# Two attentions as one pipeline, its first round inside a convolution unit, with shared norm splits: one Trainium2 core

## The reference

```python
m  = silu(c) @ w_mod + b_mod            # six modulation vectors; the same for c_ctx
h  = rms_norm(x,  norm1_g) * (1 + sc1) + sh1
hc = rms_norm(ctx, norm1_g) * (1 + csc1) + csh1      # 256 context tokens
# w_in gives, of h: gqa q, k, v; neighbourhood q, k, v; fourier; conv (a, b); 4 gates of 1024
y_gqa = gqa_latent(q, k, v, kc, vc)                  # 8 heads, 768 keys, softmax
y_na  = neighbourhood_latent(nq, nk, nv, nkc, nvc, rpb)   # 8 heads, 768 keys, bias and mask
y_fn  = fft2(fourier part, real); y_cv = silu(rms_norm(conv31(a * sigmoid(b)) + conv_b))
y  = sum_i sigmoid(gate_i) * (y_i @ w_branch[i])
x  = x + g1 * (y @ w_out)
h2 = rms_norm(x, norm2_g) * (1 + sc2) + sh2
x  = x + g2 * moe(h2)                   # router, top-2 of 16, gated experts; then the second block
```

## Time and profile before

| | us |
|---|---|
| median of 3 runs | 2862.1 (2860.08 to 2864.87) |
| the profiled execution | 2859.26 |
| its span | 2857.4 |
| TensorE busy | 2606.0 (91%) |
| VectorE busy | 1779.2 (62%) |
| ScalarE busy | 1196.3 (42%) |

### The profile page before, as it was taken

One profiled execution on the slowest core, in us unless ns is written; L12 is line 12 of the kernel. 1 busy time (PEld: TensorE's weight loads), 2 busy tenths in 40 slices (PEclk: granted clock), 3 DMA queues, 4 the chain that ended last, 5 costly groups with the idle time before them and its releaser, 6 DMA issues.

```text
span 2857.4 us, 32148 instructions
## 1 busy us (share of the span) xinstructions
PE 2606.0 (91%) x11723; PEld 2015.3 (71%) x11723; DVE 1779.2 (62%) x2639; ACT 1196.3 (42%) x1698; POOL 152.3 (5%) x186
## 2 busy tenths in 40 slices
PE   5799799899985799999698889999999898999998
PEld 2676667677674687888576656888887665688886
DVE  5465466576767698999638775444443777544445
ACT  4332255454432477777432164322233316432222
POOL 0110000000000111111101000000000010000000
PEclk8899999999998899999899999999999998999999
DMA  6456533542541699999423341332323334232322
GB/s 211 159 195 213 149 106 94 142 122 68 184 164 72 240 372 373 370 357 348 166 91 113 98 121 63 103 103 88 103 90 98 102 91 139 65 103 90 102 88 81
DMA packets 229562, 431.57 MB, mean 151 GB/s; under 512 B 63380, under 2 KB 86435, under 8 KB 229442
## 3 DMA queue, kind: packets, MB, share of 16 engines
q1 hardware_dynamic: 212210, 386.98, 40.8%
q0 software_dynamic: 17232, 43.02, 4.5%
HBM read 399.00 MB, written 46.68 MB: 156 GB/s over the span
## 4 chain that ended last, share of the span: by engine, by line
PE 55%; DVE 12%; DMA 7%; ACT 4%; issue 2%; SPq 0%; DVEq 0%; POOL 0%; ACTq 0%; POOLq 0%
PE BKP L810 25%; PE BKP L831 4%; PE BKP L832 4%; PE BKP L830 4%; PE BKP L1015 3%; DVE WL L2883 2%; DMA G<-in_w_expert_gu_dram 2%; PE BKP L1140 2%; DMA W<-in_w_expert_gu_dram 2%; PE BKP L1059 1%; ACT WH L1892 1%; DVE hL L2883 1%; DVE G L2997 1%; PE SCP L1368 1%; DVE TOP L2995 1%
## 5 line engine op out<-in xcount | busy, mean ns | idle before, releaser
L2131 DVE TENSOR_TENSOR WL<-W,WH 128x2048 fp32r<-128x2048 f32 x126 | 288.6, 2292 | 355.0 <-ACT WH L1489 353.1
L1489 ACT ACTIVATE WH<-W 128x2048 fp32r<-128x2048 f32 x126 | 241.0, 1914 | 629.6 <-PE BKP L810 319.7
L810 PE MATMUL BKP<-hH,WH 128*128 128x512 f32 x896 | 357.3, 399 | 24.5 <-DVE WL L2131 8.8
L810 PE MATMUL BKP<-hH,WL 128*128 128x512 f32 x896 | 351.9, 393 | 0.0
L810 PE MATMUL BKP<-hL,WH 128*128 128x512 f32 x896 | 351.8, 393 | 0.0
L810 PEld LDWEIGHTS BKP<-hH,WH 128*128 128x128 f32 x896 | 170.3, 190 | 72.0 <-issue 17.2
L832 PE MATMUL BKP<-WH,aL 128*128 128x512 f32 x512 | 199.2, 389 | 0.0
L830 PE MATMUL BKP<-WH,aH 128*128 128x512 f32 x512 | 199.2, 389 | 0.0
L831 PE MATMUL BKP<-WL,aH 128*128 128x512 f32 x512 | 199.2, 389 | 0.0
L810 PEld LDWEIGHTS BKP<-hL,WH 128*128 128x128 f32 x896 | 170.1, 190 | 36.4
L810 PEld LDWEIGHTS BKP<-hH,WL 128*128 128x128 f32 x896 | 170.4, 190 | 34.1
(11 more groups left out here) (547 smaller groups left out, 5547.8 us busy)
## 6 DMA issues: line engine op xcount, KB each, us to landing
W<-in_w_expert_gu_dram SPq DMA_DIRECT2D x46, 1024.0 KB, 7.5
G<-in_w_expert_gu_dram SPq DMA_DIRECT2D x46, 1024.0 KB, 7.5
W<-in_w_in_dram SPq DMA_DIRECT2D x42, 1024.0 KB, 5.2
W<-in_w_up_dram SPq DMA_DIRECT2D x32, 1024.0 KB, 5.2
W<-in_w_down_dram SPq DMA_DIRECT2D x32, 1024.0 KB, 5.0
W<-in_w_expert_down_dram SPq DMA_DIRECT2D x24, 1024.0 KB, 6.6
G<-in_w_expert_down_dram SPq DMA_DIRECT2D x22, 1024.0 KB, 6.8
X<-in_w_mod_dram SPq DMA_DIRECT2D x16, 1024.0 KB, 6.0
```

Of the source, the lines that this page charges most:

```text
L810: mm = pe.matmul(BK[j][:, 0:cols], lt, rh, start=start and a == 0, stop=stop and a == len(q) - 1, skip_group_check=True)
L1489: act.activation(WH[s][:], W[s][:] if raw is None else raw, ACT.Copy).then_inc(sems["w_hi"], 1)
L2131: v.tensor_tensor(WL[s][:], W[s][:] if raw is None else raw, WH[s][:].bitcast(F32), ALU.subtract).then_inc(sems["w_lo"], 1)
```

## The change

1. **First norm.** A new `affine_split` replaces the split of x. ScalarE now applies scale and shift itself, twice from the same PSUM tile: once into hH, once into F. VectorE only subtracts. ScalarE waits for hL of tile k - 2 before it overwrites F. The split of the context keeps its form. VectorE's WL of unit 1 moves ahead of the scaling of x.
2. **Context keys.** The transposes of the context keys move from ahead of unit 4 to behind its first group. `begin` moves into the evacuation, behind the weight splits (`begun`), and ScalarE's high part of unit 5 moves ahead of the key copies.
3. **Late sums and loads.** Both `late_sums` are cut into four sums, one behind each group of units 18 and 20. SyncE loads unit 20 ahead of the late units 8 to 12 and unit 21 ahead of 13 to 15. ScalarE splits unit 19 within the Fourier stage. VectorE makes WL of unit 19 behind the fourth Fourier step and WL of unit 20 behind late unit 13.
4. **First attention inside unit 21.** VectorE's first gate remainders and the first head's remainders move into `conv_in`, ahead of its bank work. ScalarE makes the first head's high parts as soon as unit 20 is done. TensorE makes scores 0 without waiting for the banks.
5. **One pipeline.** The second attention takes over from the first without running empty. The first call's last pair already makes the high parts, remainders, scores and maximum of the second call's first rounds, and the second call's round 0 finishes the first call's last pair.
6. **Second norm and router.** `affine_split` again. After each tile VectorE does one of the eight h2 operations (into ST, no longer in place). TensorE gets 48 extra transposes into an unused bank ahead of L1293 and 52 ahead of the first gathered rows (`warm`).

```diff
@@ SyncE @@
             blk(w, 3328)
-            for u in range(8, 2 * NLATE):
+            unit(w[0:UN, 2816:2816 + UN])
+            for u in range(8, 13):
                 late_unit(u)
-            blk(w, 2816)
+            unit(w[UN:2 * UN, 2816:2816 + UN])
+            for u in range(13, 2 * NLATE):
+                late_unit(u)
@@ TensorE @@
-            pe.wait_ge(sems["tm_ready"], T.next("tm_ready"))
-            turn("sink", cols_of(TM), NC, 1)
-            blk(cx, "T", UN, 2)
+            def keys_turned(j):
+                if j == 0:
+                    pe.wait_ge(sems["tm_ready"], T.next("tm_ready"))
+                    turn("sink", cols_of(TM), NC, 1)
+            unit(cx, 0, "T", UN, True, False, 2, each=keys_turned)
+            unit(cx, 4, "T", UN, False, True, 2)
...
-            blk(h, "F")
-            late_sums(4)
-            blk(h, "F")
+            unit(h, 0, "F", UN, True, False, each=late_sums(0))
+            unit(h, 4, "F", UN, False, True)
+            unit(h, 0, "F", UN, True, False, each=late_sums(4))
+            unit(h, 4, "F", UN, False, True)
...
+                if joined:
+                    body(False, False, IDN)
+                else:
+                    scores(0)
+                    for b in BANKS:
+                        pe.wait_ge(sems[b], T.at(b))
+                    pe.sem_inc(sems["head_o"], 2)
+                    T.skip("head_ptc:full", 2)
+                    scores(1)
+                    body(True, False)
...
+            def warm(count):
+                for _ in range(count):
+                    pe.transpose(BK[3][:, 0:P], IDN[:], IDN[:])
@@ ScalarE @@
+            def affine_split(ks, scale, bias):
+                for k in ks:
+                    act.wait_ge(sems["norm_tr"], T.next("norm_tr"))
+                    src = TP[:, (k % 2) * 512:(k % 2) * 512 + S]
+                    act.activation(hH[:, k, :], src, ACT.Identity, scale=scale(k), bias=bias(k))
+                    if k >= 2:
+                        act.wait_ge(sems["norm_lo"], T.next("norm_lo"))
+                    act.activation(F[:, k % 2, :], src, ACT.Identity, scale=scale(k), bias=bias(k)).then_inc(sems["norm_free"], 1)
...
+            unit()
             kv_sink(NC, "st_filled0")
-            s = begin(STORES_1, "ctx_nv")
-            blk(copies(lambda j: ST[0][:, j, :], UN, 2, "st_filled0"))
+            unit(begun(STORES_1, "ctx_nv", copies(lambda j: ST[0][:, j, :], UN, 2, "st_filled0")))
...
+                if not final:
+                    act.wait_ge(sems["gemm_done"], T.at("gemm_done:w", 4))
+                    rounded(0)
+                    act.wait_ge(sems["head_go"], T.next("head_go"))
@@ VectorE @@
+            def affine_split(ks, beside=None):
+                for k in ks:
+                    v.wait_ge(sems["norm_free"], T.next("norm_free"))
+                    v.tensor_tensor(hL[:, k, :], F[:, k % 2, :], hH[:, k, :].bitcast(F32), ALU.subtract).then_inc(
+                        sems["norm_lo"], 1)
+                    if beside:
+                        beside(k)
...
             for g in range(4):
                 fourier(g)
-                late(8 + g)
-            for u in range(12, 2 * NLATE):
+                if g < 3:
+                    late(8 + g)
+            unit()
+            for u in range(11, 14):
                 late(u)
-            blk()
-            late_columns(4)
+            unit()
+            skip_banks()
+            late_columns(0)
+            late(14)
+            late(15)
...
             def conv_in():
+                late_columns(4)
+                v.wait_ge(sems["gemm_done"], T.at("gemm_done:out", 0))
+                for q in range(4):
+                    gate_lo(0, q)
+                remainders(0, SCALE)
                 for j in range(4):
```

More of the change, by code:

```diff
@@ L299, in program @@
         Y2 = flat(G[:]).rearrange("p (t d) -> p t d", t=NT)
+        H2 = [flat(ST[i // 2][:])[:, i % 2 * D:i % 2 * D + D] for i in range(NT)]
         SIG, HID = QS[0][:], F[:, 0, :]
@@ L962, in late_sums, with go @@
             def late_sums(first):
-                for i in range(first, first + 4):
+                def go(b):
+                    i = first + b
+                    if i == 4:
+                        pe.wait_ge(sems["mod_out"], NMOD + 1)
                     pe.wait_ge(sems["mod_lo"], 2 * NMOD + 2 * (i + 1))
@@ L1018, in gates, with attend @@
                     mm.then_inc(sems["side_mm"], 1)
-            def attend(count, loads, keys, PTB, read, eye, beside=None):
+            def attend(count, loads, keys, PTB, read, eye, beside=None, joined=False):
                 chunks = lambda n: range(0, keys(n % NT), 512)
@@ L1091, in body @@
                             values(0, not first)
-                for b in BANKS:
-                    pe.wait_ge(sems[b], T.at(b))
-                pe.sem_inc(sems["head_o"], 2)
-                T.skip("head_ptc:full", 2)
-                scores(0)
-                scores(1)
-                body(True, False)
+                if joined:
[8 more added lines that the diff above has]
+                    body(True, False)
                 pe.sem_inc(sems["paused"], 1)
-                if count > 4:
-                    T.loop(count // 2 - 2, lambda i: body(False, False))
+                if not joined:
+                    T.loop(count // 2 - 1, lambda i: body(False, False))
+                    return
+                T.loop(count // 2 - 2, lambda i: body(False, False))
                 body(False, True)
@@ L1681, in conv_gate @@
                     act.activation(CT[:, j, :], BK[j], ACT.Sigmoid).then_inc(sems[BANKS[j]], 1)
-            blk(conv_gate)
+            unit(conv_gate)
+            for b in BANKS:
+                T.skip(b)
             blk(None, False)
@@ L2442, in body @@
                             v.wait_ge(sems["head_exp"], T.next("head_exp"))
-                        if n + 1 < 2 * NT or not last:
-                            top((n + 1) % (2 * NT), bias if n + 1 < 2 * NT else bias_next)
+                        if n + 1 < 2 * NT:
+                            top(n + 1, bias)
+                        elif not last:
+                            top(0, bias_next)
                         if tt == NT - 1:
                             inverse(s)
-                        if beside:
-                            beside(i, n)
+                        beside(i, n)
@@ L2456, in attend @@
-                v.sem_inc(sems["head_go"], 1)
-                T.skip("head_o", 2)
-                remainders(0)
-                top(0, bias)
-                if other is None:
-                    body(0, True, False, bias, bias)
-                else:
-                    body(0, True, False, bias, bias)
-                    body(1, False, False, bias, other)
-                    bias = other
-                done = 1 if other is None else 2
+                            put(*ahead)
+                if bias is None:
+                    v.wait_ge(sems["w_lo"], T.at("w_lo", 0))
+                    v.sem_inc(sems["head_go"], 1)
+                    T.skip("head_o", 2)
+                    top(0, None)
+                    body(0, None, first=True)
+                else:
+                    body(0, (1, pairs - 1))
@@ L2467, in attend @@
                 v.sem_inc(sems["paused"], 1)
-                T.loop(count // 2 - 1 - done, lambda i: body(i + done, False, False, bias, bias))
-                body(count // 2 - 1, False, True, bias, bias)
+                T.loop(pairs - 2, lambda i: body(i + 1, (stage, i)))
+                if bias is None:
+                    body(pairs - 1, (stage, pairs - 2), bias_next=na_bias)
+                    return
+                body(pairs - 1, (stage, pairs - 2), last=True)
                 v.wait_ge(sems["head_exp"], T.next("head_exp"))
-                factors_in(count // 2 - 1)
@@ L2472, in attend @@
-                put(count // 2 - 1)
+                factors_in(stage, pairs - 1)
+                put(stage, pairs - 1)
                 v.wait_ge(sems["head_y"], T.at("head_y", 0))
@@ L2501, in conv_taps @@
                 return go
-            for q in range(4):
-                gate_lo(0, q)
-            attend(8, lambda tt: KEYS, None, 1, 0, beside=conv_taps(0))
             def mixed_remainders(s, l):
```

171 lines of the change are left out of this document (91 added, 80 removed).

## The result

The changed kernel takes 2817.12 us (median of runs from 2812.72 to 2821.18) where the kernel before takes 2861.09 (2859.23 to 2864.87): 44 us shorter, a ratio of 0.9859, interval 0.984 to 0.9877. The forecast was 2810, range 2801 to 2827, so it saved 7 us less than forecast. The profiled execution took 2814.46 us (span 2812.6), 44.8 less than that of before; the sum had said 50.2.

The account below looks back on a forecast made before the run. TensorE was taken as the bound, so edits pay only where it idles or runs at the lower clock. Four places, 13.1 + 19.7 + 11.6 + 5.8 = 50.2, from 2859.3 gave 2809.1, forecast 2810; range 2801 to 2827.

Parts of the forecast that it names:

- Place 1: First norm and context units, up to unit 6: -13.1 us, between -10.5 and -14.5; nothing changes from unit 6 to 17.
- Place 2: Fourier stage, convolution and first scores: -19.7 us, between -14 and -22, of which 19.1 up to scores 0.
- (a): Without the first late sums ahead, unit 18 starts near 275.4 instead of 280.61: 4.5 us of sums, less VectorE's hold.
- The 0.6 us set down for the ramp: First attention's first rounds at 2.4 GHz: 0.6 us more saved, on top of 19.1.
- Place 3: Junction of the two attentions, joined into one pipeline: 101.64 - 90.04 = -11.6 us, between -6 and -12.
- The bias tile's 3 us of cover: Bias tile wanted near 523 in the first attention's last round, its loads landing at 518 to 520: hidden by 3 us.
- Place 4: Second norm and router: -5.8 us, between -1.5 and -8.5, with 3.5 from h2 rows leaving the path.
- The placement at 1.8 us: L1293's 16 matmuls, 3.61 us at 1.2 GHz before, take about 1.8 with 48 transposes ahead.
- A: Rival: transposes don't raise the clock, L1293 stays at 3.6 us; Place 4 gives -2, total 2814; chance 0.12.
- B: Rival: bias tile, heads' loads or context store late; Places 1 to 3 give 10.5, 14, 6; 2823 us; chance 0.17.
- C: Rival: TensorE waits in unit 20 for the last late sums; Place 2 gives -5, total 2825; chance 0.05.
- D: Rival: joined pipeline's pair period grows from 45.02 us; slower from 51.3, or 2874 at 1 us per round; chance 0.03.

## Why the prediction was right, and where it was off

**The total**: within the range, and nearer to the forecast than the mechanism was. At the second tile's first expert wait, behind all four places, the profiled execution is 38.9 us ahead, where the sum had 50.2. The 5.9 us that it gains after that come from stages of the same code, in a trace whose rest is the shortest of eleven; that is luck.

**What bounds the kernel**: right. The join's 11.7 us, taken away again, were missing in full at the output units behind it. The prediction's first reading, TensorE 55% of the chain's span, was of a chain that breaks off at 534.53 us; nothing in the sum rests on it.

**Place 1** failed by 7.0 us, in two terms. The first is the date of the store, in the sentence "the copies end near 96.5, the store near 105.1". The copies ended at 97.22, 0.7 us later than that, and the store ended 11.24 us behind them and not 8.56: 2.7 us more, nearly all in the transfers (10.5 us from the first issue, 7.9 before). I had taken the duration from a row beside which nothing else was in the queues, without asking what would now be in them: unit 7's weights wait for the WL of unit 5, the change makes it sooner, the late units stand behind them in SyncE's list, and so 3 MB went out from 96.68 on and not from 110.87. My lower bound, "the store lands no sooner than before" (106.61), was no bound: it landed at 108.46. ScalarE's wait ended at 108.46 instead of 105.1, and unit 6 came at 109.15 instead of 105.8. The run with the later loads put it at 106.89. The second term was costed at nothing: "from unit 6 to 17 nothing changes". The order did not, but the clock did. Unit 6 began behind a 3.88 us gap at half clock, where before it followed unit 5 without one, and units 6 to 9 took 45.3 us and not 43.7. Around the turn's gap, as long as it was (4.24 and 4.28 us), the clock fell sooner and came back later: it was at 0.50 from about 156.8 to 167.0 us, where before it was so from about 167.3 to 170.8. The transposes and units 10 to 13 cost 2.1 us more. 3.35 + 1.6 + 2.1 = 7.05. The filling of that second gap gave 3.05 us. What decides how long the half clock lasts behind a gap of the same length the runs do not say: the placement, behind idle times of 1.3 to 2.5 us, took 1.96 or 1.97 us in some kernels and 2.8 to 3.0 in others.

The passes on ScalarE were sized right: 0.78 us each, where I had 0.7 to 0.8. The Trainium skill ("ScalarE: Activation LUTs", section "What ACT_TABLE_LOAD costs") has about 93 ns for each pointer operand, and the estimate from it was 0.78.

**Place 2**: 19.35 us against 19.1 for the scores. No gap ahead of unit 19, the late sums inside the units, no window at 0.50 in between. In (a) the reason given and the date don't fit: 4.5 us of sums, less something, can't move unit 18 by the 5.2 us written, and it moved by 5.9. The 0.6 us set down for the ramp went the other way: the first twelve gate matmuls took 4.3 us (324.10 to 328.42), most of them at half clock, where the run with the late loads later took 2.7.

**Place 3**: 11.6 us, forecast and measured twice. The bias tile's 3 us of cover held.

**Place 4**: 4.0 against 5.8 in this trace, 5.3 to 5.9 in four others of the same code. The move of the h2 rows and the split did what was written: from the second norm to the placement it took 37.51 us and not 40.95, 3.4 less against the 3.5 forecast. The placement at 1.8 us came out in two traces of five (1.96, 1.97); in the changed kernel's, the 48 transposes raised the clock, the 2.48 us gap behind them was followed by its fall, and the placement took 2.99. The same happened ahead of the experts: in the three dearer of the five traces' first expert stretches (16.5 to 16.9 us, against 15.3 in the other two and 15.3 without extra transposes) the gap behind the second batch cost more than the 0.5 us allowed.

**Rivals.** A had the mechanism wrong (transposes do raise the clock), and its 2 us for this place are below all five traces. B came nearest: one of its transfers, the context store, was late, by 3.4 us with the copies ahead of it; the bias tile and the heads' loads were not. But B had 10.5 us for place 1, and 6.1 is far less: the late store alone leaves 9.75, and neither B nor the range had a term for the clock. C and D did not happen; the pairs' period is 45.02 as before.

## What to carry to other kernels

When a step is made earlier, list what stands behind it in every other engine's list: a load that was held back by chance comes forward with it and may share the DMA engines with the very transfer that the step waits for. Here two loads stood behind a third that had waited for the step, and moving them behind the next load took a few lines. A gap of TensorE costs its length and often a stretch at half clock behind it (1.6 us behind the 3.88 us gap, none behind the one of 1.34), and transposes of an idle bank that ran in the gap to its end held the clock where I read it. They gave 3 us at the one gap weighed alone; put behind a wait that ends late they cost 2.6 and 5.2 us. Where one stage varies by 6 us between executions, read changes of 3 us at landmarks ahead of it, and a stretch of 70 us in more than one trace: of the same code it varied by 2 us.

## What was not expected of the hardware

- 3 MB of loads issued 0.9 to 1.3 us ahead of a store (1.57 MB in the queue) went with 6.6 us to landing for the 128 KB pieces of its values instead of 3.6; with 2 MB of them issued 8 us later it was 4.1.
- Extra transposes raised the granted clock to 0.92 and 0.86 and, in gaps filled to the end, held it at 1.00; followed by gaps of 1.3 to 2.5 us they gained between 0 and 1.9 us in sum, in five traces.
- Two gaps of the same length (4.28 and 4.24 us) behind full-clock work had the clock fall 4.7 us after the start of the one (kernel before) and 2.3 us after that of the other (changed kernel).
- The expert stage, at a DMA share near 1.00, took 423.1 to 429.5 us over eleven executions of the same code, and what follows it, at a DMA share near 0.3 in the stretches shown, 1459.6 to 1468.2.
